# Seven block products for eight in the MLP's up projection, with the weight sums formed by DRAM-to-DRAM transfers

## What is computed

```python
x = x + ox @ w_co                       # end of cross-attention
hm = _rmsnorm(x, g_mlp)
x = x + jnp.square(jax.nn.relu(hm @ w_up)) @ w_down   # w_up 1024x4096, w_down 4096x1024
y = _rmsnorm(x, g_final)
```

## Time and profile before

| | |
|---|---|
| three runs, us | 2278.52, 2278.54, 2279.7; median 2278.54 |
| profiled execution, span | 2278.1 us |
| PE busy | 2227.6 us, 98% of the span |
| DVE, ACT, POOL busy | 944.3, 462.1, 554.3 us |
| DMA, mean | 75 GB/s |

### The profile page before, as it was taken

One profiled execution on the slowest core, in us unless ns is written; L12 is line 12 of the kernel. 1 busy time (PEld: TensorE's weight loads), 2 busy tenths in 40 slices (PEclk: granted clock), 3 DMA queues, 4 the chain that ended last, 5 costly groups with the idle time before them and its releaser, 6 DMA issues.

```text
span 2278.1 us, 47875 instructions
## 1 busy us (share of the span) xinstructions
PE 2227.6 (98%) x21034; PEld 2105.9 (92%) x21034; DVE 944.3 (41%) x1185; ACT 462.1 (20%) x875; POOL 554.3 (24%) x288
## 2 busy tenths in 40 slices
PE   8999999999999999999999999999999999999998
PEld 6899888888888899889999988999999999999997
DVE  5333644637455354354453163544114304412523
ACT  4111434224242211253111032110000000000011
POOL 0232201101010122122332201333333323323331
PEclk9999999999999999999999999999999999999999
DMA  7211101112020193236113143111111111111112
GB/s 283 85 38 45 64 19 55 40 39 69 19 65 30 42 283 114 94 142 247 46 37 120 37 148 140 46 37 46 46 42 41 47 46 46 38 46 46 46 37 88
DMA packets 57694, 170.88 MB, mean 75 GB/s; under 512 B 8416, under 2 KB 24160, under 8 KB 54752
## 3 DMA queue, kind: packets, MB, share of 16 engines
q1 hardware_dynamic: 46816, 143.63, 18.4%
q10 hardware_dynamic: 10752, 25.35, 3.2%
HBM read 140.90 MB, written 28.05 MB: 74 GB/s over the span
## 4 chain that ended last, share of the span: by engine, by line
PE 88%; DVE 4%; DMA 3%; ACT 2%; SPq 1%; issue 1%; POOL 0%; ACTq 0%; DVEq 0%; POOLq 0%
PE ps L402 87%; DMA w_raw<-w 2%; DVE F L1207 1%; SPq L2293 1%; ACT F L1815 1%; DVE Xst L1207 1%; DMA vc<-vc 1%; DVE F L1210 0%; DVE F L1213 0%; DVE Sst L1210 0%; ACT L1815 0%; DMA par<-par 0%; POOL w_split L393 0%; PE ps L1077 0%; DVE F L1387 0%
## 5 line engine op out<-in xcount | busy, mean ns | idle before, releaser
L402 PE MATMUL ps<-A_s,w_split 128*128 128x364 f32 (+1 forms) x6192 | 1082.3, 333 | 8.0 <-ACT zstg L1815 6.5
L402 PEld LDWEIGHTS ps<-A_s,w_split 128*128 128x128 f32 x6192 | 1029.7, 189 | 35.5 <-issue 15.2
L402 PE MATMUL ps<-B_s,w_split 128*128 128x364 f32 (+3 forms) x4032 | 672.4, 328 | 0.3 <-POOL w_split L393 0.3
L402 PEld LDWEIGHTS ps<-B_s,w_split 128*128 128x128 f32 x4032 | 667.7, 188 | 3.5 <-issue 1.1
L390 POOL CAST w_split<-w_raw 128x1024 fp32r<-128x1024 f32 x142 | 151.6, 1067 | 1678.2 <-PE ps L402 1589.1
L393 POOL TENSOR_TENSOR w_split<-w_raw,w_split 128x1024 fp32r<-128x1024 f32 x142 | 402.5, 2835 | 11.4
L1207 DVE TENSOR_TENSOR F<-ps,F 128x1092 f32<-128x1092 f32 (+3 forms) x52 | 62.8, 1208 | 420.6 <-PE ps L402 420.6
L1815 ACT ACTIVATE B_s<-T 128x1092 fp32r<-128x1092 f32 x32 | 35.9, 1121 | 621.6 <-DVE T L1213 621.6
L1213 DVE SCALAR_TENSOR_TENSOR T<-ps,rsx 128x1092 f32<-128x1092 f32 x32 | 41.5, 1296 | 205.2 <-PE ps L402 197.2
L1207 DVE TENSOR_TENSOR B_s<-T,B_s 128x1092 fp32r<-128x1092 f32 x32 | 105.9, 3309 | 1.1
L1207 DVE TENSOR_TENSOR T<-T 128x1092 f32<-128x1092 f32 x58 | 104.1, 1795 | 1.6 <-ACT T L1815 0.4
(11 more groups left out here) (214 smaller groups left out, 1857.0 us busy)
## 6 DMA issues: line engine op xcount, KB each, us to landing
w_raw<-w SPq DMA_DIRECT2D x144, 512.0 KB, 3.5
z<-zstg SPq DMA_DIRECT2D x83, 182.0 KB, 1.9
F<-z SPq DMA_DIRECT2D x16, 546.0 KB, 7.9
w_raw<-w SPq DMA_DIRECT2D x7, 1024.0 KB, 10.2
kc<-kc SPq DMA_DIRECT2D x7, 1024.0 KB, 4.8
vc<-vc SPq DMA_DIRECT2D x7, 1024.0 KB, 4.8
F<-x SPq DMA_DIRECT2D x8, 546.0 KB, 9.6
Zs<-z SPq DMA_DIRECT2D x16, 273.0 KB, 20.0
```

Of the source, the lines that this page charges most:

```text
L402: return pe.matmul(out, lhsT, rhs, start=start, stop=stop, skip_group_check=skip)
```

## The change

It replaces the up projection's plain products by a seven-product scheme for 2x2 blocks. A **quad** is two output tiles of 128 features times all 1088 tokens: contraction in two halves of 512, tokens in two halves of 544 (`HT`), output tiles r = 0, 1. Plain block products would be eight a quad (2 x 2 x 2); here there are seven products of one block (128 output features, 512 of the contraction) with one token half, each 4 x 3 x 2 = 24 matmuls of 272 columns.

- **Token side.** `xb` and `xt` (hi and lo) hold the seven moving operands, four of which are plain blocks, differences or sums of F blocks times the gain. They are formed once, at the end of attention, on DVE and ACT (`difference`, `mlp_lo`, `mlp_hi`, `tok_sums`, `tok_hi`).
- **Weight side.** Three of the seven stationary operands are plain blocks. Four kinds are sums of two to four blocks of w_up. They are formed in DRAM (`sums_up`): 16 plain transfers and 28 accumulating ones of 1 MB each, issued from POOL after each second slot of the merge and output projections. POOL waits for all earlier ones before each later stage (`sums_step`).
- **PSUM.** Products P1 and P2 add up in banks 0 and 1, P5 and P3 in banks 3 and 4, P6, P7 and P4 in banks 6 and 7. ACT copies P1 and P5 out half-way (`kept`), DVE forms their sum and the four output blocks (`u2`, `c11`, `c22`, `c12`, `c21`).
- **Weights.** All MLP weights now stream in units of 4 contraction tiles (256 KB) through a ring of four. POOL makes hi alone, DVE makes lo (`unit_lo`). 11 x 16 = 176 units: 112 products and 64 half slots of the down projection.
- **Groups.** A down slot is split into halves over the contraction: after each two quads all 8 output tiles get 36 matmuls and one addition to F. 64 additions instead of 32.

```diff
@@ POOL
-            with pool.Fori(0, (SLOTS - S_PW) // 2) as i:
+            def sums_step(stage, groups):
+                if stage:
+                    pool.wait_ge(d_sum, 16 * issued[0])
+                for g in groups:
+                    if stage == 0:
+                        for kind in range(4):
+                            to_sum(g, kind, 1, 0, False)
+                    if stage == 1:
+                        for kind in (0, 1, 3):
+                            to_sum(g, kind, 1, 1, True)
+                        to_sum(g, 2, 0, 0, True)
+                    if stage == 2:
+                        to_sum(g, 1, 0, 0, True)
+                        to_sum(g, 3, 0, 0, True)
+                    if stage == 3:
+                        to_sum(g, 3, 0, 1, True)
+            def to_sum(g, kind, r, half, add):
+                if add:
+                    pool.dma_start(sum_block(g, kind), up_block(g, r, half), accum_op=ALU.add).then_inc(d_sum, 16)
+                else:
+                    pool.dma_start(sum_block(g, kind), up_block(g, r, half)).then_inc(d_sum, 16)
+                issued[0] += 1
...
+            for i in range((S_CQ - S_MIX) // 2):
+                for b in range(2):
+                    split(S_MIX - S_PW + 2 * i + b, b)
+                sums_step(i // 2, (2 * (i % 2), 2 * (i % 2) + 1))
...
+            def pair(i, o, first, last):
+                for l in range(PAIR_UNITS):
+                    pool.wait_ge(d_m[l % 4], i * 176 + (D_M + 176 * o + 16 * (l // 4) + 16))
+                    if first and l < 4:
+                        pool.wait_ge(g_done, C_CO + 7 + l // 2)
+                    else:
+                        pool.wait_ge(m_used, i * PAIR_UNITS + (BEFORE + PAIR_UNITS * o + l - 3))
+                    pool.sem_inc(w_taken, 1)
+                    pool.tensor_copy(msp[:, l % 4, 0, :, :], mraw[:, l % 4, :].rearrange("p (k n) -> p k n", k=4)).then_inc(m_hi, 1)
@@ PE
-            first_pair(S_MLP, A_s, (h_ready, 18), 4)
-            for g in range(4):
-                plain(S_MLP + 16 * g, u + 16 * g, 8, A_s, hold=(h_ready, 18), skip=0 if g else 2)
-                plain(S_MLP + 16 * g + 8, u + 16 * g + 8, 8 if g < 3 else 6, B_s, hold=(up_s, g * 8))
+            ORDER, ORDER_FIRST = (1, 5, 6, 2, 7, 3, 4), (1, 5, 2, 3, 6, 7, 4)
+            def quad(i, o, first, q):
...
+                    pe.wait_ge(m_ready, i * PAIR_UNITS + (BEFORE + PAIR_UNITS * o + l + 1))
+                    for k in range(4):
+                        for m, (wp, xp) in enumerate(((0, 0), (0, 1), (1, 0))):
+                            for c in range(2):
+                                last = mm(ACC_OF[p][:, c, :], msp[:, l % 4, wp, k, :], X_OF[p][:, k, xp, HC * c:HC * c + HC],
...
+                    if first and q == 0 and p == 5:
+                        second_root()
@@ DVE, end of attention
             for k in range(KT):
                 v.wait_ge(g_done, u + k + 1)
                 tt(tri(F[:, k, :]), G[k % 2], tri(F[:, k, :]), ALU.add).then_inc(g_free[k % 2], 1)
+                if k < 4:
+                    difference(k)
                 if k:
-                    residual(k - 1, 16, "gmlp", A_s)
-            residual(KT - 1, 16, "gmlp", A_s)
+                    mlp_lo(k - 1)
+                if k == KT - 1:
+                    for l in range(2):
+                        v.wait_ge(m_hi, BEFORE + l + 1)
+                        tt(msp[:, l, 1, :, :].rearrange("p k n -> p (k n)"), mraw[:, l, :],
+                           f32(msp[:, l, 0, :, :]).rearrange("p k n -> p (k n)"), ALU.subtract).then_inc(m_ready, 1)
+            mlp_lo(KT - 1)
@@ DVE, a quad that isn't the first
+                unit_lo(i, o, l0 + 4)
+                unit_lo(i, o, l0 + 5)
+                both_sums()
+                u2()
+                unit_lo(i, o, l0 + 6)
+                c11()
+                own.wait()
+                unit_lo(i, o, l0 + 7)
+                c22()
+                hidden_lo(i, n, q, 0, 0, 0)
+                unit_lo(i, o, l0 + 8)
+                c12()
+                hidden_lo(i, n, q, 1, 1, 1)
+                unit_lo(i, o, l0 + 9)
+                c21()
+                hidden_lo(i, n, q, 2, 0, 1)
+                unit_lo(i, o, l0 + 10)
+                hidden_lo(i, n, q, 3, 1, 0)
@@ SP, after the slots of S_CO
-            with sp.Fori(0, (SLOTS - S_CO - 2) // 2) as i:
+            with sp.Fori(0, (S_MLP - S_CO - 2) // 2) as i:
                 for b in range(2):
                     load_slot(i, b, S_CO + 2)
+            sp.wait_ge(d_sum, 16 * 44)
```

More of the change, by code:

```diff
@@ L1175, in chunk_sum, with pair_of_groups @@
+            def pair_of_groups(i, o, first, last):
+                for d in range(2):
+                    for q in (2 * d, 2 * d + 1):
+                        quad(i, o, first, q)
+                    down(i, o, d, 6 if last and d == 1 else 8)
+            pair_loop(pe, pair_of_groups)
             def chunk_sum(c):
@@ new lines, in down @@
+            def down(i, o, d, tiles, last):
+                f0 = 16 * o + 8 * d
+                for t in range(tiles):
+                    l = down_unit(d, t)
+                    v.wait_ge(m_used, i * PAIR_UNITS + (BEFORE + PAIR_UNITS * o + l + 1))
+                    tt(tri(F[:, t, 0:T + 4]), G[t % 2], tri(F[:, t, 0:T + 4]), ALU.add).then_inc(m_f, 1)
+                    if not (last and d == 1 and t >= 4):
+                        unit_lo(i, o, l + 4)
+                    if last and d == 1 and t:
+                        rms_add(t - 1, 24, Tn)
@@ new lines, in _, with pair_of_groups @@
+            tok_sums()
+            v.wait_ge(rs_ready, 4)
+            def pair_of_groups(i, o, first, last):
+                for d in range(2):
+                    for q in (2 * d, 2 * d + 1):
+                        quad(i, o, first, q)
+                    down(i, o, d, 6 if last and d == 1 else 8, last)
+            QUAD_STEPS = 1
+            pair_of_groups(0, 0, True, False)
+            with v.Fori(0, 2) as i, own.loop(i, 2, 4 * QUAD_STEPS):
+                pair_of_groups(i, 1, False, False)
```

402 lines of the change are left out of this document (342 added, 60 removed).

## The result

The changed kernel takes 2445.11 us (median of 4 runs, 2443.13 to 2448.43) against 2278.53 us before: ratio 1.0728, 95% interval 1.0713 to 1.0744. It is slower, as forecast, but by 167 us instead of 33, and far outside the range of 2260 to 2372. Its profiled execution has a span of 2441.1 us at a mean granted clock of 0.959, against 2278.1 us.

The account below looks back on a forecast made before the run. PE, busy 98% of the span, was taken to bound the kernel. From 2278.1 us, -37.0 (up products), +14.0 (MLP start), +52 (transfers) and +4 (clock) gave 2311 us; range 2260 to 2372, likeliest case 2295 to 2330.

Parts of the forecast that it names:

- Term 4: Merge and output projections: POOL, waiting for DMA transfers, delivers splits late and PE loses time, +52 us.
- the two ends that I had named: Price of a 1 MB copy from DRAM to DRAM: one pass, 2.53 us, or two, 5.05 us.
- The rule that I weighed: A reduce step runs at half a copy's rate, through two read descriptors per chunk; additions then take two passes, stall 52 us.
- Steps five to eight: Later stages of forming the weight sums, with 4, 4, 2 and 2 additions, said to fit into 24 us each.
- The sign: Whole kernel: slower by more than 0.2% (4.6 us), chance 0.68; faster by more than that, 0.22.
- three passes, or copies of two: Rival on the transfers: additions at 7.6 us, total 2367 us, with copies of 5.05 us 2407; chance 0.19.
- What I had named as proof against me: Includes the DMA share falling far below 1.0 before POOL's waits end, in the merge and output projections.
- Term 1: MLP up products: 168 matmuls of 272 columns a quad at 128.5 ns each, 21.6 us a quad, -37 us.
- Term 2: Other engines in the MLP's steady state: DVE, POOL and ACT work hides under PE's, 0 us.
- Term 3: Start of the MLP: PE waits for DVE's operands before the first product, P6, P7, P4 and the next quad, +14 us.
- Term 5: Granted clock: matmuls may run at half speed for some microseconds after each long PE wait, +4 us.

Follow-up runs that it names:

- alone_16384: Only the transfers, without the rest of the changed kernel, with a descriptor reserve of 16384 bytes a partition instead of 2048; the 8 whole additions took 44.6 us.

## Why the forecast was wrong, term by term

| term | forecast, us | measured in the profiled execution, us |
|---|---|---|
| up products | -37 | -45 |
| other engines in the steady state | 0 | +1.4 |
| start of the MLP | +14 | +22 |
| end of the MLP | none | +3 |
| PE's wait for w_split | +52 | +169 |
| clock behind the waits | +4 | +10 |
| sum | +33 | +161 |

The two profiled executions lie 163.0 us apart; the last 2 us are not assigned.

**Term 4 failed, in the model of the queue.** The price of an addition was right, 5.05 us (5.09 measured). That of a copy, 2.53 us, was too low but within the two ends that I had named: 8 in 28 us at 295 GB/s in alone_16384, 3.5 us each, some 16 us over the 16 copies (339 GB/s from 1103 to 1112 in the kernel). The rule that I weighed, from the Trainium skill, "Collectives: The Full Stack", section "The bandwidth ceiling: the fold count and why AG ≠ RS ≠ AR", gives the right price here, by way of the load's rate: an addition moves at 206 GB/s, about half of the 415 GB/s of the earlier trace rows. Against a copy from DRAM to DRAM, and the rule compares with a copy, it is 0.70 (295 GB/s) or 0.61 (339), not half, and no run here shows the two read descriptors. What failed is the queue taken for a stream: I let POOL issue at 0.70 us each, as ACT does, and let transfers follow without a gap. In fact one addition leaves at a time: 28 x 8.9 us instead of 28 x 5.05, and POOL, which PE needs every 11.95 us, is blocked while it lasts. Steps five to eight I had fitting into their 24 us each. Steps five and six, four additions each, take some 39 us, and PE waits 14.15 and 12.87 us behind them; only seven and eight, two each, fit. The sign came out right, but not by the wait that I had priced, that of POOL for all earlier transfers: the trace nowhere shows POOL released by one. The text of the rival "three passes, or copies of two" names an issue that is too long ("if POOL needed over 3 us for an issue"), at 2367 and 2407, and gives it 0.19 together; at 9 us an issue it comes to more than either. That an engine can be held by an issue with no wait in its code was the case I didn't price. The earlier trace rows showed ACT's queue, another kind, and no row of before showed a transfer issued by POOL at all: this unknown had no upper bound in the trace, and the range should have said so.

What I had named as proof against me came true: the DMA share fell far below 1.0 before POOL's waits ended (0.73 and 0.71 in the two stretches of eight additions).

**Term 1** was right in mechanism and small by 8 us: a product takes 3.01 us, not 3.08, 125.6 ns a matmul instead of the 128.5 interpolated from the earlier trace rows; two quads and the halves of eight down slots take 90.10 us. PE's timeline, one product and the next:

```profile
1734.07 3.18 PE L516 MATMUL ps<-xt,msp 128*128 128x272 f32 x24
1737.09 3.18 PE L516 MATMUL ps<-xb,msp 128*128 128x272 f32 x24
```

**Term 2** was right: PE has no wait inside a quad; the 1.2 us at 2062.71 is at the turn of the loop.

**Term 3** was right in mechanism and too small. P1 began 4.55 us late (4.8 forecast) and P6 3.80 (4.5). But P7 waited 7.6 us instead of 2.8, since its bank is freed by u2 (over at 1713.4, P7 begins at 1713.49), which stands behind both token splits, p5s, c11 and a lo on DVE; I had traced what P7 reads and not what it writes. And PE worked slower behind each wait, 4.57 us for 24 matmuls instead of 3.18: the granted clock was 0.82 from 1682 to 1720.

**The end of the MLP** I hadn't looked at: from the root of the first piece to the end of the span it takes 22.5 us with 36 product matmuls in it, 26.0 before with 84. The 48 that are gone were worth 24 x 158 + 24 x 112 ns = 6.5 us, so 3 us are lost, as less work lies beside the last roots.

**Term 5** is 10 us instead of 4, as there were six long waits and not three or four. The granted clock reads 0.50 while PE waits (1054 to 1070), its level of 1.2 GHz. 144 matmuls take 24.06 us at full clock and 25.4 to 26.6 behind a wait.

## What to carry to other kernels

A transfer that POOL issues costs POOL's time, not only the queue's: if its descriptors don't fit behind those that the reserve has been given since it was last started afresh, the engine stands until all that is under way has been moved. So count rows, those of transfers long done too, and put such transfers one to a slot, where POOL and the weight loads both have room. For a step that no row of the trace shows, price the case in which nothing overlaps before the one in which all of it does. When a bank is reused, trace what frees it as well as what fills it.

## What the hardware showed that I had not expected

- How many transfers POOL issued in a row followed their rows and the size of the reserve: with 2048 bytes one addition of 512 rows, or three of 256, or three copies of 512; with 4096 three additions or seven copies of 512; with 16384 eight copies and eight additions, and then seven halves.
- Room came back only when all that was under way had been moved, even where most of the reserve belonged to transfers long done: POOL's next issue comes within 2 us of that, and the engines are empty for 2 to 3 us.
- An addition from DRAM to DRAM moves at 205 to 214 GB/s with rows of 2 or 8 KB alike, and at 169 GB/s with rows of 1 KB.
- Products with 272 columns run at 125.6 ns a matmul, a little below the line between 232 and 344 columns (128.5).
